# Routing of a mixture-of-experts block: a wait in the queue of weight loads, a reordered count on VectorE, and fewer idle products

## What is computed

```
g_idx = argmax(v @ w_rg + b_rg)                    # one of 4 groups
top_v, top_i = top_k(expert logits in the group, 2)
gate = softmax(top_v) * p_group
# tokens are sorted by expert into blocks of rows
def run(tok_b, e):
    a, u = split(v_pad[tok_b] @ w_e_in[e])         # 1024 -> 2 x 512
    return (silu(a) * u) @ w_e_out[e]              # 512 -> 1024
out[token] += run(...) * gate
```

## Time and profile before

| | before |
|---|---|
| median of 3 runs | 2727.82 us (2725.1 to 2729.26) |
| profiled execution, own time | 2725.17 us |
| its span | 2723.9 us |
| TensorE busy | 2627.2 us (96%) |
| VectorE busy | 1286.9 us (47%) |
| ScalarE busy | 898.7 us (33%) |
| granted clock of TensorE, mean | 0.993 |
| DMA traffic | 381.62 MB, mean 140 GB/s |

### The profile page before, as it was taken

The page is one execution under the profiler, slowest core; times in us unless marked ns, Lnnn a source line. Parts: engine busy times, 40 slices in busy tenths (PEclk is TensorE's granted clock), DMA queues, the critical chain, the costliest instruction groups (busy, mean ns, idle before and its releaser), DMA issues.

```text
span 2723.9 us, 38632 instructions
## 1 busy us (share of the span) xinstructions
PE 2627.2 (96%) x16282; PEld 2065.9 (76%) x16282; DVE 1286.9 (47%) x2277; ACT 898.7 (33%) x1328; POOL 148.7 (5%) x201
## 2 busy tenths in 40 slices
PE   8999999999999989999999999999999999999997
PEld 6778888778744333349999999988879786788885
DVE  4445666534423333356344465544544434644444
ACT  4334555333221111123222243444444322432222
POOL 0000000000100000000000000031230400000000
PEclk9999999999899999999999999999999999999998
DMA  3012212144599999963222222211111222322221
GB/s 144 16 64 66 61 58 62 58 140 139 218 414 420 421 420 421 420 285 117 94 86 94 81 76 83 96 59 51 59 59 44 66 93 87 103 99 93 93 90 57
DMA packets 78203, 381.62 MB, mean 140 GB/s; under 512 B 9944, under 2 KB 10200, under 8 KB 52816
## 3 DMA queue, kind: packets, MB, share of 16 engines
q1 hardware_dynamic: 71856, 357.14, 35.7%
q0 software_dynamic: 5456, 20.11, 1.9%
q10 hardware_dynamic: 720, 1.90, 0.2%
HBM read 372.67 MB, written 10.62 MB: 141 GB/s over the span
## 4 chain that ended last, share of the span: by engine, by line
PE 74%; DMA 8%; DVE 4%; SPq 2%; ACT 2%; issue 1%; DVEq 0%; ACTq 0%
PE ps L208 72%; DMA rmore<-in_w_ein 5%; DMA ring<-in_w_ein 2%; SPq L293 2%; PE ps L212 1%; DVE ringr L581 0%; PE ps L1963 0%; DMA ring<-in_w_hg 0%; ACT L218 0%; ACT ringr L575 0%; DVE hT L2666 0%; DVE uT L472 0%; ACT hdd L1230 0%; DVE hT L3958 0%; DVE mgb L3955 0%
## 5 line engine op out<-in xcount | busy, mean ns | idle before, releaser
L208 PE MATMUL ps<-uh,ringr 128*128 128x264 f32 (+1 forms) x2256 | 553.8, 340 | 4.4 <-DVE uTr L619 2.4
L208 PEld LDWEIGHTS ps<-uh,ringr 128*128 128x128 f32 x2256 | 366.6, 189 | 48.7 <-DVE uTr L619 3.6
L208 PE MATMUL ps<-buh,ringr 128*128 128x512 f32 (+1 forms) x1312 | 347.2, 351 | 4.4 <-ACT hg L1212 3.3
L208 PE MATMUL ps<-uTr,ringr 128*128 128x512 f32 (+1 forms) x1136 | 350.5, 345 | 0.0
L581 DVE TENSOR_TENSOR ringr<-ring,ringr 128x1024 fp32r<-128x1024 f32 (+1 forms) x215 | 258.2, 1212 | 141.2 <-ACT ringr L575 140.6
L575 ACT CAST ringr<-ring 128x1024 fp32r<-128x1024 f32 (+1 forms) x215 | 219.4, 1036 | 92.8 <-DMA ring<-in_w_fi 34.3
L208 PEld LDWEIGHTS ps<-buh,ringr 128*128 128x128 f32 x1312 | 218.9, 189 | 35.5 <-issue 7.4
L208 PEld LDWEIGHTS ps<-uTr,ringr 128*128 128x128 f32 x1136 | 197.4, 189 | 22.5 <-issue 3.1
L208 PE MATMUL ps<-ful,ringr 128*128 128x264 f32 (+1 forms) x648 | 169.9, 323 | 0.2 <-DVE ful L508 0.2
L208 PE MATMUL ps<-fhh,ringr 128*128 128x264 f32 (+1 forms) x576 | 123.7, 321 | 0.0
L2627 DVE TENSOR_TENSOR fsg<-ps,fsg 128x528 f32<-128x528 f32 (+1 forms) x44 | 30.8, 700 | 193.5 <-PE ps L208 189.7
(11 more groups left out here) (485 smaller groups left out, 4553.5 us busy)
## 6 DMA issues: line engine op xcount, KB each, us to landing
rmore<-in_w_ein SPq DMA_DIRECT2D x51, 1024.0 KB, 27.0
eahead<-in_w_ein SPq DMA_DIRECT2D x47, 1024.0 KB, 26.7
ring<-in_w_ein SPq DMA_DIRECT2D x30, 1024.0 KB, 27.0
rmore<-in_w_eout SPq DMA_DIRECT2D x27, 1024.0 KB, 27.0
ring<-in_w_fi SPq DMA_DIRECT2D x54, 512.0 KB, 3.7
ring<-in_w_eout SPq DMA_DIRECT2D x19, 1024.0 KB, 27.3
eahead<-in_w_eout SPq DMA_DIRECT2D x18, 1024.0 KB, 27.3
fmore<-in_w_fi SPq DMA_DIRECT2D x34, 512.0 KB, 3.7
```

Of the source, the lines that this page charges most:

```text
L208: return self.P.matmul(out, lhsT, rhs, start=start, stop=stop, skip_group_check=True)
```

## The change

Three edits:
- On VectorE the wait for `pick.at(2)` with its four copies and `meta_dve` moves behind the count of blocks, so the count comes in front of that wait.
- On SyncE, ahead of the load of expert 2's fourth input chunk, a wait for the four stores of the rows. It holds this load and all behind it. (In the loop's own order this is the ninth load.)
- The idle products in front of expert 0's transposes go from 11 to 6.

```diff
@@ place_dve
         V.tensor_scalar(self.pair, k.ps[:, b, 0:NE // 2], -1.0, float(S), MUL, ADD).then_inc(self.given.next(), 1)
-        V.wait_ge(*self.pick.at(2))
-        over = k.ps[0:64, b + 1, NBLK:NBLK + NOV]
-        V.tensor_scalar(self.more, over, -1.0, float(S), MUL, ADD).then_inc(self.given.next(), 1)
-        V.tensor_scalar(self.tokens, over, -1.0, float(S), MUL, ADD).then_inc(self.given.next(), 1)
-        V.tensor_copy(self.gates, k.ps[:, b + 1, 0:NBLK]).then_inc(self.given.next(), 1)
-        self.nxt.meta_dve()
         V.tensor_tensor(self.cmp, end[0:1].unsqueeze(1).to_broadcast([1, NOV, 32]),
                         iota[0:1, 0:NOV].unsqueeze(2).to_broadcast([1, NOV, 32]), ALU.is_le).then_inc(s.next(), 1)
...
         V.tensor_copy(self.ov[:, 0:1], end[0:1, 31:32]).then_inc(self.blocks.next(), 1)
+        V.wait_ge(*self.pick.at(2))
+        over = k.ps[0:64, b + 1, NBLK:NBLK + NOV]
+        V.tensor_scalar(self.more, over, -1.0, float(S), MUL, ADD).then_inc(self.given.next(), 1)
+        V.tensor_scalar(self.tokens, over, -1.0, float(S), MUL, ADD).then_inc(self.given.next(), 1)
+        V.tensor_copy(self.gates, k.ps[:, b + 1, 0:NBLK]).then_inc(self.given.next(), 1)
+        self.nxt.meta_dve()
@@ Experts.sp
                     if 4 * e + c < EARLY:
                         continue
+                    if (e, c) == (2, 3):
+                        after(k.SP, *(r.last() for r in self.route.rows))
                     k.load(k.a["w_ein"][e, c], 2048, self.into.at(4 * e + c + 1))
@@ Experts.pe
-        self.k.busy(6, 11)
+        self.k.busy(6, 6)
```

## The result

| | before | after |
|---|---|---|
| median of 20 runs each | 2725.92 us | 2729.77 us |
| lowest to highest | 2723.71 to 2729.26 | 2725.32 to 2732.67 |
| profiled execution, own time | 2725.17 us | 2730.12 us |
| its span | 2723.9 us | 2728.8 us |

The ratio is 1.0013, with a 95% interval of 1.0008 to 1.0019: the change costs 3.5 us (2.2 to 5.2). That is less than the 0.2% that the prediction took for the least a measurement can tell; with 20 runs of each kernel the interval still lies wholly above 1, so the change does cost time. The profiled execution of after is 5.0 us longer than that of before, a little more than the runs differ.

The account below looks back on a forecast made before the run. The expert stage was taken to end with a weight stream paced by expert 0's first chunks. Later gather +0.5, transposes +0.3, lower clock +2.4 and the rest 0 gave +3.2 us: 2731.0 us, range 2725 to 2735.

Parts of the forecast that it names:

- What sets the end of the stage: Expert stage: each microsecond by which expert 0's first chunks are used up later moves the stage's end by about one.
- The stores gain nothing: Row stores before the first gather: holding two loads leaves their landing as it is, gain 0, at most 0.5 us.
- third rival: Row stores: with loads sharing engines equally, rows land some 4 us earlier, giving 2726.2 or 2723.8 us; chance 0.08.
- The gather gets later: First gather, beside the released loads: 6.4 us instead of 5.5, so expert 0's transposes start 0.5 us later.
- The idle products: TensorE before expert 0's transposes: 12 records take 2.7 us, then 4.1 us idle until the gather lands.
- The cover that goes: Expert 0: after the shorter burst the lower clock costs +0.3 us in the transposes, +2.4 us in the first products.
- The first rival: Expert 0's start: the clock doesn't matter and transposes follow the gather alone, -0.4 or +0.5, about 2727.9 us; chance 0.18.
- The count is hidden: VectorE's block count, moved into its wait: ends in idle time in front of the gather, so this edit costs 0.
- The second rival: First gather: caught behind the two released loads, it takes 10.1 us; +6.8 us in all, 2734.6 us; chance 0.14.

Follow-up runs that it names:

- e9: The changed kernel, but SyncE's held loads wait for both first gathers to land instead of the four stores; ratio to before 0.9997 (0.9988 to 1.0006).
- e12: The changed kernel with SyncE's held loads waiting for the first gather alone, and 11 idle products instead of 6; ratio to before 0.9995 (0.9986 to 1.0004).
- e7: The changed kernel with SyncE's wait three chunks earlier, ahead of expert 2's first chunk, holding five loads; ratio to before 1.0008 (0.9999 to 1.0018).
- e11: The changed kernel with SyncE's held loads waiting for the first gather alone to land, 6 idle products; ratio to before 0.9999 (0.9990 to 1.0008).
- e1: The kernel before with only the idle products cut from 11 to 6; ratio to before 1.0010, 2.7 us slower (0.3 to 5.2).
- e4: The changed kernel with 18 idle products instead of 6; ratio to before 1.0006 (0.9997 to 1.0015).
- e8: The changed kernel with 26 idle products instead of 6; ratio to before 1.0010 (1.0001 to 1.0019).
- e5: The changed kernel without its wait on SyncE, 6 idle products; ratio to before 1.0007 (0.9998 to 1.0016), 1.9 us slower.
- e10: The changed kernel with expert 2's first chunk waiting for the four stores and its fourth for the first gather; ratio to before 1.0007 (0.9998 to 1.0016).

## Why the prediction came out as it did

The forecast was +3.2 us, 2731.0 us; measured were +3.5 us (2.2 to 5.2) and 2729.77 us, since the 20 runs of before lie 1.9 us under the three it started from. The mechanism was right in the main; that the sum came so close is partly luck. In the profile its terms up to the end of expert 0 come to +4.4 us (15.57 to 19.93) instead of +3.2, and the stage to +5.2, more than the runs' middle of 3.5. By its steps:

- **What sets the end of the stage.** Right. SyncE's waiting load went out 2.61 us later, the one behind it 3.61 us later (750.14 against 746.53), and the end of the stage followed, 4.62 us later. The last microsecond is a term that the sum lacked: the clock fell a second time, 0.52 from 756 to 759, and the sixth load after the restart went out 4.94 us late, at 761.81 instead of 756.87. Counted from the last store, the end of the stage moved as the end of expert 0's products did to within 1.2 us in every kernel but e9 and e12 (1.9 us more), where the held loads and a second fall of the clock came in between.
- **The stores gain nothing.** Right: 12.79 us from issue to landing against 13.0. The third rival falls with it; e7 shows which loads would have had to go.
- **The gather gets later.** The direction was right, the size not: 7.07 us against the 6.4 taken, so that the transposes started 1.2 us later behind the stores' landing and not 0.5. The picture behind it, a gather that moves beside the loads from the start, failed: for 4.3 us no packet of the gather moved, and in the kernel before none for 2.6 us. In e11, with no load moving, the first packet came 1.7 us after the issue, so that much is the gather's own. The Trainium skill, "DMA: Bandwidth & Descriptors", section "Queues, rings and completion order", says that a DMA engine changes in turn between the queues it has work for; the stores show it, and so does the gather once it moves (35 packets beside 46); its first 4.3 us don't, and whether it had work in its queue by then no run shows.
- **The idle products.** Mis-sized: 12 records took 1.58 us and not 2.7, as the clock had not yet fallen when they ran in this execution. The pause was 5.93 us instead of 4.1; what that alone changed no run shows.
- **The cover that goes.** Right, and the largest term: 2.74 us in the products against 2.4, 0.37 in the transposes against 0.3. The first rival (the clock is no matter) is out by e1, which has nothing but the shorter burst: it needed a kernel no slower than before, and the interval is 0.3 to 5.2 us slower. That the lower clock is the cause is shown by the record lengths in the profile of each kernel (7.09 only where the pause was under 0.5 us, 8.45 or more where it was 1.5 us or more); the times show a loss for the shorter burst, while filling the pause (e4, e8) gave no gain that they can tell.
- **The count is hidden.** Wrong as it was put. With 6 idle products it makes no difference that the runs can tell (e5 against e1, 1.0007 and 1.0010), for the pause is there anyway; alone it opens a pause of 2.06 us. The prediction had looked at who waits for the count, and not at what ends earlier when its waiter starts earlier.
- **The second rival** had the right mechanism, loads released ahead of the gather, and too high a price for this place; e7 and e10 show its price, 8.5 to 8.9 us, where more loads are released.

The three parts alone cost 2.7, 0.8 and 2.5 us, 6.0 in all, and together 3.5; the intervals are too wide to show a difference. In the profiles each of the three opens a pause and pays for the lower clock by itself, while the changed kernel pays for it once in expert 0.

Two limits remain. A single profile says little about a difference of a few microseconds: over the fourteen profiles here the part behind the last weights, which no edit touches, takes 1530.0 to 1535.2 us; up to its last 20 us the clock falls there not at all in e11 and three times in e10. And why a gather behind released loads starts moving 2.7 us later than one without them (4.4 against 1.7 us) is open.

## What to carry to other kernels

Before filler work in front of a wait is cut or moved earlier, look at what ends the wait: if that doesn't move, the filler's end only opens a pause, and the products behind it can run at the lower clock. A wait that holds bulk loads back for the sake of a small transfer has to hold them until that small transfer has landed, not until the one before it has; and what is held then stands in front of the loads that follow (e9). Where a stream of loads sets the end of a stage, cost an edit by what it does to the stream's restart. Before a difference between two profiles is put down to an edit, take off what lies ahead of and behind the part that the edit can reach.

## What was unexpected about the hardware

- The first gather (0.26 MB) took 3.3 to 3.4 us with no load released beside it (e9, e11, e12), 5.5 to 5.9 us behind loads that had been issued long before and were running out, 7.0 to 7.1 us with two loads of 1 MB issued about a microsecond ahead of it, and 8.5 to 8.9 us with three or five issued up to 3 us ahead. Part of this is the time to its first packet: 1.7 us after the issue with no load moving (e11), 2.6 before, 4.4 in the changed kernel. After that it shared the engines with the loads packet by packet, as the row stores did.
- In all six profiles with a pause of 1.5 to 2.2 us in front of the eight transposes, the granted clock was 0.50 in a part of expert 0's products, which then took 1.4 to 2.6 us more; in five of them it was still 1.00 through the transposes.
- The last of four row stores of 512 KB landed in 12.6 to 13.0 us after its issue in the twelve kernels that hold back two loads or none, and in 6.6 and 6.8 us in the two that hold five (e10, e7).
